# Retention on split fp32r operands, keys first, with the first norm computed beside the modulation

## The chip, the cores and the metric

The kernel runs on one core of one Trainium2 chip. The metric is the device time of one execution in microseconds (us). A run gives several executions, and their median counts.

## The reference

A four-layer diffusion-style model over 512 image tokens and 256 context tokens with 1024 features, all in fp32. Each layer has an adaptive modulation (six vectors from a conditioning vector), an RMS norm, a mixer, a second RMS norm and a gated feed-forward part. The mixer of layer 0 is windowed attention, that of layer 1 is bidirectional retention, those of layers 2 and 3 are mixed. The change touches the retention and the first norm of the program. Cut to these:

```python
h_x = modulate(rms_norm(x, norm1_g[i]), mx[0], mx[1])      # x * rsqrt(mean(x*x) + eps) * g, then h * (1 + scale) + shift
# retention, per head (4 heads, 256 key features, 512 value features), T = 512 image + 256 context tokens
q, k = rope_2d(q), rope_2d(k) * 256 ** -0.5                # context keys are not rotated
scores = einsum('bnhd,bmhd->bhnm', q, k) * decay           # forward and backward decay, gamma_h ** |n - m|
o = einsum('bhnm,bmhe->bnhe', scores, v)                   # keys and values of the image and of the context
mu = mean(o, -1); var = mean(square(o - mu), -1)
y = (o - mu) * rsqrt(var + EPS) * gn_gain
out = (silu(g) * y) @ w_o
```

## The kernel before, in words

Activations lie with features on the 128 partitions and tokens along the free axis. Weights come in units of 128x1024 (512 KB): the queue of SyncE loads unit u into `WR[u % 2]`, ScalarE rounds it to fp32r into `WH[u % 2]` (`refill`, line 684), VectorE takes the rest into `WL[u % 2]` (`refill`, line 1031), and TensorE multiplies. A product of a split weight and a split activation takes three fp32r passes, WH x HH, WH x HL, WL x HH (`product`, line 313; two outputs at once in `product_pair`, line 331; with activations as the stationary side and value rows as the outcome in `product_rows`, line 344). `refill(u)` on ScalarE waits for the load and for product u - 2, so each unit is split while the one before it is multiplied. Every engine runs its instructions in the order in which its program was written, with semaphores between them; this order is written out by hand in one function per engine.

**Retention** (lines 487, 852, 1257, 1550 for TensorE, ScalarE, VectorE, GpSimd) takes 16 units per head: 2 for the queries (512 tokens), 2 for the keys (768 tokens), 2 gates, 4 for the values (6 tiles of 128 tokens, 8 k steps), 2 gates, 4 for the output product. Keys and queries are rotated on VectorE (`rope`, six operations). Scores and values are plain fp32 matmuls: 12 for the scores (line 513) and 24 for the values (line 521), which the trace shows as two records each. VectorE multiplies the scores by the decay (line 1312) as it takes them out of PSUM. After the values ScalarE copies four tiles `rO` out, TensorE averages them over the features with a matrix of 1/512 (line 527, 4 fp32 matmuls), VectorE subtracts the mean (line 1315), ScalarE squares, TensorE averages the four squares (line 532, 4 matmuls), with the third gate's product between the two averages. Then come the fourth gate's product, the reciprocal root with a Newton step (`rsqrt` line 700, `newton` line 1080), the product with the gate on GpSimd (line 1555), the scaling (1322) and the split into `rYH` (ScalarE, 891) and `rYL` (VectorE, 1326), and the output product (line 548), whose result VectorE adds to X (line 1333, event `r_out`). The next head's first product waits for `r_out` of the last unit.

**First norm and modulation** (end of each program function). The first 4 x 2 pieces of the modulation weights, 1 MB each, are loaded into two buffers, a piece of part nb waiting for the matmul of part nb - 1 that read its buffer. X (3 MB) is loaded behind the first two pieces. After the fourth part TensorE turns the row results into columns (`ada_turn`), ScalarE squares the eight tiles of X, TensorE sums them as they come (line 388, 8 x 128x768 in fp32), and `norm` (lines 716 and 1086) follows: reciprocal root, Newton step, eight tiles scaled on VectorE (1108, 1111), modulated on ScalarE (725, 728, 732) and split on VectorE (1095, 1098). The first product pair takes the tiles as they come. In all later norms GpSimd sums the squares (line 1528) and TensorE takes two matmuls (line 382).

Of the kernel before, what the change touches and what calls it, by code (L numbers as in the profile page):

```python
# [6 lines left out]
ALU = mybir.AluOpType  # L7
ACT = mybir.ActivationFunctionType
F32 = mybir.dt.float32
# [5 lines left out]
P = 128  # L15
# [19 lines left out]
NB = 5 * P + 1  # L35

# [51 lines left out]
class Memory:  # L88
# [49 lines left out]
    def first_ada(self):  # L138
        t = self.tile
        self.AR0 = [t(f"AR0{i}", [P, 4, 512]) for i in range(2)]  # L140
        self.EV0 = t("EV0", [P, 512])
# [40 lines left out]
    def retention(self):  # L182
        t = self.tile
        self.rQ = t("rQ", [P, 2, S])
        self.rK = t("rK", [P, 2, T])
        self.rV = t("rV", [P, 6, 512])
        self.rG = t("rG", [P, 4, S])
        self.rO = t("rO", [P, 4, S])
        self.rAT = t("rAT", [P, 6, S])
        self.rYH = t("rYH", [P, 4, S], F32R)  # L190
        self.rYL = t("rYL", [P, 4, S], F32R)
# [6 lines left out]
        self.rDS = self.rO[:].rearrange("p a b -> p (a b)")[:, 0:NU]  # L198
        self.rTMP = self.rAT[:].rearrange("p a b -> p (a b)")[:, 0:NU]
# [46 lines left out]

HEADS = 6 * 16
# [62 lines left out]
def tensor_program(PE, M, on, FIRST):  # L310
    PS, HH, HL, WH, WL = M.PS, M.HH, M.HL, M.WH, M.WL

    def product(u, dst, src, nk, segs, after=None, ready=None, between=None):
# [5 lines left out]
        for k in range(nk):  # L319
            if between and k == 3:  # L320
                between()
# [22 lines left out]
    def product_rows(u, nk, k0, width, tiles, dst, first, last, ready=None, paired=False):  # L344

        PE.wait_ge(*on("w_lo", u))
        for at in range(nk * len(tiles)):
# [3 lines left out]
            for i, (h, w) in enumerate(((HH, WH), (HH, WL), (HL, WH))):  # L351
                mm = PE.matmul(dst(m), h[:, k0 + k, m * P:(m + 1) * P], w[u % 2][:, k * width:(k + 1) * width],  # L352
                               start=(first and k == 0 and i == 0 and not (paired and m % 2)),
                               stop=(last and k == nk - 1 and i == 2 and not (paired and m % 2 == 0)))
        mm.then_inc(*on.up("product", u))

    def ada_sum(l, nb, buf, before):
        for half in range(2):
            PE.wait_ge(*on(f"ada_load{half}", (l, nb)))
# [17 lines left out]
    def mean_square(tag, segs, summed):  # L377
        if summed:
            for i, t in enumerate((M.WK[2], M.WK[1])):
                PE.wait_ge(*(on("squared", (tag, KT - 1)) if i else on("square_summed", (tag, KT - 2))))  # L380
                for a, b, _ in segs:
                    mm = PE.matmul(PS[2][:, a:b], M.ONE[:, :], t[:, a:b], start=(i == 0), stop=(i == 1))
            mm.then_inc(*on.up("mean_square", tag))
            return
        for k in range(KT):
            PE.wait_ge(*on("squared", (tag, k)))
            for a, b, _ in segs:
                mm = PE.matmul(PS[2][:, a:b], M.ONE[:, :], M.WK[k % 2][:, a:b], start=(k == 0), stop=(k == KT - 1))
            if k < KT - 1:
                mm.then_inc(*on.up("square_taken", (tag, k)))  # L390
        mm.then_inc(*on.up("mean_square", tag))
# [95 lines left out]
    def retention():  # L487
        vb = [bank(PS, m) for m in range(6)]
        for h in range(4):
            u = FIRST["ret"] + 16 * h  # L490
            after = ("r_out", (h - 1, 3)) if h else None
            if h == 0:
                product_pair(u, PS, IMG, ("h_lo", "1a"))
            else:
                product(u, PS[0], (HH, HL), KT, IMG, after)
                product(u + 1, PS[1], (HH, HL), KT, IMG)
            product(u + 2, PS[2], (HH, HL), KT, ALL)
            product(u + 3, PS[3], (HH, HL), KT, ALL)
            for e in range(2):
                product(u + 4 + e, PS[e][:, 512:1024], (HH, HL), KT, IMG)  # L500
            PE.wait_ge(*on("r_rope", (h, 1)))
            PE.wait_ge(*on("r_gate", (h, 1)))
            for n in range(4):
                product_rows(u + 6 + n, 2, 2 * n, 512, range(6), lambda m: vb[m], n == 0, n == 3)
            for m in range(6):
                d = PS[(3, 0)[(m % 4) // 2]][:, 512 * (m % 2):512 * (m % 2) + 512]
                if m > 3:
                    PE.wait_ge(*on("r_decayed", (h, m - 4)))
# [1330 lines left out]
```

## Time and profile before

| | |
|---|---|
| median of 3 executions | 3689.19 us (3688.10 to 3695.85) |
| the profiled execution, its time | 3685.29 us |
| its span in the trace | 3684.0 us |
| granted TensorE clock, mean | 0.963 |
| TensorE matmuls busy | 3449.4 us (94%) |
| VectorE, ScalarE, GpSimd busy | 1743.7, 1214.7, 255.6 us |
| DMA | 334.24 MB, mean 91 GB/s |

The span runs from the first to the last instruction of the profiled execution; 1.3 us lie around it. A share of busy time is an average over all stages. The chain that ended last names, at each moment, the instruction on which everything behind it waited. Matmul records overlap: a pass that takes a new place every 0.2275 us has a record of 0.39 us, so stretches of the chain tell what a pass costs and the mean of a record does not.

### The profile page before, as it was taken

The page shows a single profiled execution, that of the slowest core. Times are in us where ns is not written, and L with a number is a line of the kernel's source. Part 1 is how long each engine was busy: PE and PEld are TensorE (multiplying, and loading weights), DVE is VectorE, ACT ScalarE, POOL GpSimd, SP SyncE. Part 2 cuts the span into 40 slices and gives each one's busy share as a digit, 9 for nine tenths or more (in the row PEclk, how much of TensorE's full clock was granted, in tenths as well). Part 3 has the DMA queues.
Part 4 walks back from the last instruction along what each step waited for, and adds up shares of the span by engine and source line. Part 5 has one row for each costly group of instructions (what it writes and reads, how often), then busy time and mean ns, then how long its engine had stood idle before and what let it go on. Part 6 is the DMA issues. An engine that isn't in the chain of part 4 may idle for free.

```text
span 3684.0 us, 42824 instructions
## 1 busy us (share of the span) xinstructions
PE 3449.4 (94%) x17952; PEld 2782.0 (76%) x17952; DVE 1743.7 (47%) x2627; ACT 1214.7 (33%) x1696; POOL 255.6 (7%) x337
## 2 busy tenths in 40 slices
PE   6979989999989999998999999889999989979998
PEld 3767778888865756656888786578888878568886
DVE  3567454333343333426757425546535433644343
ACT  4357442112232221224222424442212233543232
POOL 0101100000100000001001100010000010010001
PEclk7989999999999999999999998899999999889999
DMA  5400033323221211113544210023323322012222
GB/s 204 182 26 2 30 115 126 120 92 126 82 69 35 94 48 58 65 41 139 192 149 173 98 58 29 12 87 127 133 84 126 105 86 81 12 46 97 97 97 86
DMA packets 87776, 334.24 MB, mean 91 GB/s; under 512 B 11168, under 2 KB 14240, under 8 KB 83744
## 3 DMA queue, kind: packets, MB, share of 16 engines
q1 hardware_dynamic: 66416, 252.85, 19.3%
q0 software_dynamic: 21168, 78.65, 6.4%
q8 instruction: 142, 2.33, 0.2%
q14 instruction: 50, 0.41, 0.0%
HBM read 329.37 MB, written 2.10 MB: 90 GB/s over the span
## 4 chain that ended last, share of the span: by engine, by line
PE 89%; DVE 4%; ACT 4%; issue 1%; DMA 1%; SPq 0%; POOL 0%; DVEq 0%; ACTq 0%
PE PS L326 65%; PE PS L352 6%; PE PS L548 3%; PE PS L521 2%; PE PS L339 2%; PE PS L620 1%; PE PS L470 1%; PE PS L513 1%; PE PS L483 1%; PE PS L645 1%; PE PS L459 1%; PE PS L591 1%; DMA AR<-in_ada 1%; PE PS L632 1%; DVE dP L1450 1%
## 5 line engine op out<-in xcount | busy, mean ns | idle before, releaser
L692 ACT ACTIVATE WH<-WR 128x1024 fp32r<-128x1024 f32 (+1 forms) x376 | 419.0, 1115 | 1686.8 <-PE PS L326 1448.1
L326 PE MATMUL PS<-HH,WH 128*128 128x512 f32 (+1 forms) x3120 | 944.5, 358 | 29.7 <-DVE HL L1427 11.0
L326 PE MATMUL PS<-HL,WH 128*128 128x512 f32 (+1 forms) x3120 | 936.9, 355 | 0.0
L326 PE MATMUL PS<-HH,WL 128*128 128x512 f32 (+1 forms) x3120 | 936.6, 355 | 0.0
L1037 DVE TENSOR_TENSOR WL<-WR,WH 128x1024 fp32r<-128x1024 f32 (+1 forms) x376 | 486.0, 1293 | 928.6 <-ACT WH L692 928.2
L326 PEld LDWEIGHTS PS<-HH,WH 128*128 128x128 f32 x3120 | 514.6, 189 | 122.4 <-issue 16.6
L326 PEld LDWEIGHTS PS<-HL,WH 128*128 128x128 f32 x3120 | 514.4, 189 | 88.0 <-issue 2.2
L326 PEld LDWEIGHTS PS<-HH,WL 128*128 128x128 f32 x3120 | 513.9, 189 | 86.6
L326 PE MATMUL PS<-DH,WL 128*128 128x512 f32 (+1 forms) x1056 | 318.7, 356 | 0.0
L326 PE MATMUL PS<-DL,WH 128*128 128x512 f32 (+1 forms) x1056 | 318.7, 356 | 0.0
L326 PE MATMUL PS<-DH,WH 128*128 128x512 f32 (+1 forms) x1056 | 318.6, 356 | 0.0
L1163 DVE SCALAR_TENSOR_TENSOR X<-PS,MOD,X 128x512 f32<-128x512 f32 x96 | 60.6, 659 | 368.0 <-PE PS L326 368.0
L326 PEld LDWEIGHTS PS<-DL,WH 128*128 128x128 f32 x1056 | 174.2, 188 | 30.0
L326 PEld LDWEIGHTS PS<-DH,WL 128*128 128x128 f32 x1056 | 174.2, 188 | 30.0
L326 PEld LDWEIGHTS PS<-DH,WH 128*128 128x128 f32 x1056 | 174.1, 188 | 30.0
L1068 DVE SCALAR_TENSOR_TENSOR PS<-AT,CB 128x1024 f32<-128x1024 f32 x144 | 176.5, 1226 | 0.0
L352 PE MATMUL PS<-WH,HH 128*128 128x256 f32 (+1 forms) x416 | 142.2, 342 | 27.5 <-DVE HL L1095 15.8
L1536 POOL DMA_DIRECT2D AT<-in_adat x144 | 76.0, 528 | 1149.5 <-DVE AT L1068 574.7
L352 PE MATMUL PS<-WL,HH 128*128 128x256 f32 (+1 forms) x416 | 141.0, 339 | 0.0
L352 PE MATMUL PS<-WH,HL 128*128 128x256 f32 (+1 forms) x416 | 141.0, 339 | 0.0
L1528 POOL TENSOR_TENSOR WK<-WK,WK 128x768 f32<-128x768 f32 (+1 forms) x56 | 116.9, 2087 | 329.3 <-ACT WK L708 328.8
L767 ACT ACTIVATE DH<-WK 128x768 fp32r<-128x768 f32 (+1 forms) x88 | 65.1, 739 | 185.4 <-DVE WK L1154 185.4
(258 smaller groups left out, 3707.1 us busy)
## 6 DMA issues: line engine op xcount, KB each, us to landing
WR<-in_win SPq DMA_DIRECT2D x176, 512.0 KB, 3.5
AT<-in_adat POOLq DMA_DIRECT2D x144, 512.0 KB, 3.8
WR<-in_wdn SPq DMA_DIRECT2D x64, 704.0 KB, 4.0
WR<-in_wret SPq DMA_DIRECT2D x64, 512.0 KB, 3.6
WR<-in_zin SPq DMA_DIRECT2D x36, 512.0 KB, 3.5
AR<-in_ada SPq DMA_DIRECT2D x8, 1024.0 KB, 4.9
aV<-in_ada SPq DMA_DIRECT2D x8, 1024.0 KB, 4.9
aAR<-in_ada SPq DMA_DIRECT2D x8, 1024.0 KB, 6.5
```

Of the source, the lines that this page charges most:

```text
L326: mm = PE.matmul(dst[:, a:b], w[u % 2][:, k * P:(k + 1) * P], h[:, k, a:b], start=(k == 0 and i == 0), stop=(k == nk - 1 and i == 2))
L339: mm = PE.matmul(dst[v][:, a:b], w[(u + v) % 2][:, k * P:(k + 1) * P], h[:, k, a:b], start=(k == 0 and i == 0), stop=(k == KT - 1 and i == 2))
L352: mm = PE.matmul(dst(m), h[:, k0 + k, m * P:(m + 1) * P], w[u % 2][:, k * width:(k + 1) * width], start=(first and k == 0 and i == 0 and n ...
L521: mm = PE.matmul(d, M.rV[:, m, e * P:(e + 1) * P], M.rAT[:, m, :], start=(m == 0), stop=(m == 5))
L548: mm = PE.matmul(PS[half][:, 512 * v:512 * v + 512], wt[half][:, col:col + P], y[:, k, :], start=(k == 0 and i == 0), stop=(k == 3 and i = ...
L692: AC.activation(M.WH[u % 2][:, 0:n], M.WR[u % 2][:, 0:n], COPY).then_inc(*on.up("w_hi", u))
L767: AC.activation(M.DH[:, j, 0:n], HF[:, 0:n], COPY).then_inc(*on.up("d_hi", (l, jj)))
L1037: VE.tensor_tensor(M.WL[u % 2][:, 0:n], M.WR[u % 2][:, 0:n], M.WH[u % 2][:, 0:n].bitcast(F32), ALU.subtract).then_inc(*on.up("w_lo", u))
L1068: i = VE.scalar_tensor_tensor((PS[3], M.AT[v % 3])[j][:, :], M.AT[v % 3][:, :], 1.0, M.CB[:, j, :], ALU.mult, ALU.mult, accum_out=MOD[:, l ...
L1163: i = VE.scalar_tensor_tensor(X[:, m, a:b], PS[m % 2 if m else 2][:, a:b], MOD[:, l, 40 + m, j:j + 1], X[:, m, a:b], ALU.mult, ALU.add)
L1528: PO.tensor_tensor(WK[2][:, 0:n], WK[2][:, 0:n], WK[k % 2][:, 0:n], ALU.add).then_inc(*on.up("square_summed", (tag, k)))
L1536: PO.dma_start(M.AT[v % 3][:, :], dram["adat"][l - 1, v]).then_inc(*on.up(f"mod_load{v % 3}", (l, v), 16))
```

## The change

What it does, in the order of the work:

- **Keys first.** The units of a head start with the keys, into `PS[2]` and `PS[3]`, then the queries into banks 0 and 2, then two gates into banks 1 and 3. The first product of heads 1 to 3 waits for `r_gated` of the head before instead of `r_out`; the queries' products wait for `r_out`. In head 0 the pair that runs beside the norm is the keys' (768 tokens).
- **Three passes.** Rotated queries and keys, decayed scores and values are split into fp32r high and low parts, and scores and values are computed in 36 and 72 fp32r passes. The high parts are made on ScalarE, the low parts on VectorE.
- **Values centred at eviction.** ScalarE copies each value tile out with its row sum (`accum_out`), VectorE divides the sum by -512, ScalarE writes the centred high part, VectorE the low part. With centred values the outcome has mean zero over the features, so the average of line 527 and the subtraction of line 1315 are gone.
- **Order.** The third gate's product (u + 10) stands between scores and values; the fourth's (u + 11) follows the values, with the one variance matmul after its k = 4. ScalarE squares the four tiles straight from PSUM, VectorE adds them up; VectorE, not GpSimd, multiplies by the gate, from PSUM. The first output unit takes k in the outer place.
- **First norm.** Four modulation buffers in place of two (a load of part nb waits for part nb - 2). ScalarE squares X as soon as it is there, between the copies of the modulation parts; GpSimd sums the squares; TensorE takes the mean after the third part, before the fourth. VectorE scales five tiles before it finishes the modulation.

The core of the diff; lines taken away, which stand in the kernel above, are mostly left out, and so are the new buffers:

```diff
+RV_BANKS = (4, 5, 6, 7, 0, 2)
+RS_BANKS = (1, 3, 4, 5, 6, 7)
...
     def retention():
         for h in range(4):
+            out = lambda n: ("r_out", (h - 1, n)) if h else None
             if h == 0:
+                product_pair(u, PS[2:4], ALL, ("h_lo", "1a"))
             else:
+                PE.wait_ge(*on("r_gated", (h - 1, 3)))
+                product(u, PS[2], (HH, HL), KT, ALL)
+                product(u + 1, PS[3], (HH, HL), KT, ALL)
+            product(u + 2, bank(PS, 0), (HH, HL), KT, IMG, out(2))
+            product(u + 3, bank(PS, 2), (HH, HL), KT, IMG, out(3))
+            product(u + 4, bank(PS, 1), (HH, HL), KT, IMG)
+            product(u + 5, bank(PS, 3), (HH, HL), KT, IMG)
+            PE.wait_ge(*on("rK_lo", (h, 1)))
+            PE.wait_ge(*on("r_rope", (h, 0)))
             for n in range(4):
+                product_rows(u + 6 + n, 2, 2 * n, 512, range(6), lambda m: bank(PS, RV_BANKS[m]), n == 0, n == 3,
+                             event=(lambda m: ("v_rows", (h, m))) if n == 3 else None)
+            PE.wait_ge(*on("rQ_lo", (h, 1)))
             for m in range(6):
+                if m < 2:
+                    PE.wait_ge(*on("r_gate", (h, m)))
+                else:
+                    PE.wait_ge(*on("rV_raw", (h, m - 2)))
+                d = bank(PS, RS_BANKS[m])
                 for a in range(2):
+                    for i, (k, q) in enumerate(((M.rKH, M.rQH), (M.rKH, M.rQL), (M.rKL, M.rQH))):
+                        mm = PE.matmul(d, k[:, a, m * P:(m + 1) * P], q[:, a, :], start=(a == 0 and i == 0), stop=(a == 1 and i == 2))
                 mm.then_inc(*on.up("r_scores", (h, m)))
+            product(u + 10, bank(PS, 0), (HH, HL), KT, IMG, ("rV_raw", (h, 4)))
             for e in range(4):
+                d = bank(PS, RS_BANKS[e])
                 for m in range(6):
+                    if e == 0:
+                        PE.wait_ge(*on("rV_lo", (h, m)))
+                        PE.wait_ge(*on("rA_lo", (h, m)))
+                    for i, (v, a) in enumerate(((M.rVH, M.rAH), (M.rVL, M.rAH), (M.rVH, M.rAL))):
+                        mm = PE.matmul(d, v[:, m, e * P:(e + 1) * P], a[:, m, :], start=(m == 0 and i == 0), stop=(m == 5 and i == 2))
                 mm.then_inc(*on.up("r_values", (h, e)))
+            def variance():
+                if h == 0:
+                    PE.wait_ge(*on("step", "rON"))
+                PE.wait_ge(*on("r_square_sum", h))
+                PE.matmul(bank(PS, 6), M.rON[:, :], M.rSQ[:, 0, :], start=True, stop=True).then_inc(*on.up("r_var", h))
+
+            product(u + 11, bank(PS, 2), (HH, HL), KT, IMG, ("rV_raw", (h, 5)), None, variance, 5)
...
+                half, w = n % 2, u + 12 + n
+                PE.wait_ge(*on("w_lo", w))
+                PE.wait_ge(*(on("r_out", (h, n - 2)) if n > 1 else on("r_gate", (h, 2 + n))))
+                if n < 2:
+                    PE.wait_ge(*on("r_gated", (h, n)))
+                for at in range(8):
+                    v, k = (at % 2, at // 2) if n == 0 else (at // 4, at % 4)
+                    if n == 0 and v == 0:
+                        PE.wait_ge(*on("y_lo", (h, k)))
...
 def scalar_program(AC, M, on, FIRST, UNITS):
...
+            def high(what, a, dst):
+                AC.wait_ge(*on("r_half", (h, what, a)))
+                AC.activation(dst[:, a, 0:S], M.rST[a][:, :], COPY).then_inc(*on.up("r_hi", (h, what, a)))
+
+            refill(u + 2)
+            refill(u + 3)
             for a in range(2):
+                AC.activation(M.rKH[:, a, S:T], PS[2 + a][:, S:T], COPY).then_inc(*on.up("rK_ctx", (h, a)))
+            for a in range(2):
+                high(1, a, M.rKH)
+            refill(u + 4)
+            refill(u + 5)
+            for a in range(2):
+                high(0, a, M.rQH)
...
+            refill(u + 8)
...
+            refill(u + 9)
+            refill(u + 10)
+
+            def v_high(m):
+                AC.wait_ge(*on("rV_mean", (h, m)))
+                AC.activation(M.rVH[:, m, :], M.rVT[m % 2][:, :], IDENT, bias=M.rVM[:, m:m + 1]).then_inc(*on.up("rV_hi", (h, m)))
+
+            for m in range(6):
+                AC.wait_ge(*(on("v_rows", (h, m)) if m < 5 else on("product", u + 9)))
+                if m > 1:
+                    AC.wait_ge(*on("rV_lo", (h, m - 2)))
+                AC.activation(M.rVT[m % 2][:, :], bank(PS, RV_BANKS[m]), COPY,
+                              accum_out=M.rVM[:, m:m + 1]).then_inc(*on.up("rV_raw", (h, m)))
+                v_high(m)
+            refill(u + 11)
+            for m in range(6):
+                AC.wait_ge(*on("r_decayed", (h, m)))
+                AC.activation(M.rAH[:, m, :], M.rST[m % 2][:, :], COPY).then_inc(*on.up("rA_hi", (h, m)))
             refill(u + 12)
+            AC.activation(M.rG[:, 2, :], bank(PS, 0), ACT.Silu).then_inc(*on.up("r_gate", (h, 2)))
+            for e in range(4):
+                AC.wait_ge(*on("r_values", (h, e)))
+                AC.activation(M.rSQ[:, e, :], bank(PS, RS_BANKS[e]), SQUARE).then_inc(*on.up("r_squared", (h, e)))
+            rsqrt(("r", h), M.rVT[0][:, :], bank(PS, 6), M.rVT[1][:, :], ("r_var", h))
             refill(u + 13)
...
+    ada_copy(0, 0, M.EV0[:, :])
+    AC.wait_ge(*on("x_load", 0))
+    squares("0a", T, range(4))
+    ada_copy(0, 1, M.EV0[:, :])
+    squares("0a", T, range(4, KT))
+    ada_copy(0, 2, M.EV0[:, :])
+    root("0a", T)
+    ada_copy(0, 3, M.EV0[:, :])
     refill(0)
     refill(1)
...
 def vector_program(VE, M, on, FIRST, UNITS):
...
+            VE.wait_ge(*on("product", u + 1))
+            rope(h, 1, PS[2][:, 0:S], PS[3][:, 0:S], M.rKH, M.rKL)
+            for a in range(2):
+                VE.wait_ge(*on("rK_ctx", (h, a)))
+                VE.tensor_tensor(M.rKL[:, a, S:T], PS[2 + a][:, S:T], M.rKH[:, a, S:T].bitcast(F32),
+                                 ALU.subtract).then_inc(*on.up("rK_lo", (h, a)))
             refill(u + 4)
...
+            refill(u + 9)
+            refill(u + 10)
             for m in range(6):
+                VE.wait_ge(*on("rV_raw", (h, m)))
+                mean = M.rVM[:, m:m + 1]
+                VE.tensor_scalar(mean, mean, -1.0 / 512, None, ALU.mult).then_inc(*on.up("rV_mean", (h, m)))
+                VE.wait_ge(*on("rV_hi", (h, m)))
+                VE.scalar_tensor_tensor(M.rVL[:, m, :], M.rVT[m % 2][:, :], mean, M.rVH[:, m, :].bitcast(F32), ALU.add,
+                                        ALU.subtract).then_inc(*on.up("rV_lo", (h, m)))
+            refill(u + 11)
+            def low(m):
+                VE.wait_ge(*on("rA_hi", (h, m)))
+                VE.tensor_tensor(M.rAL[:, m, :], M.rST[m % 2][:, :], M.rAH[:, m, :].bitcast(F32),
+                                 ALU.subtract).then_inc(*on.up("rA_lo", (h, m)))
+
+            for m in range(6):
...
+                if m > 1:
+                    low(m - 2)
+                    VE.wait_ge(*on("rA_lo", (h, m - 2)))
                 VE.wait_ge(*on("r_scores", (h, m)))
+                VE.scalar_tensor_tensor(M.rST[m % 2][:, :], bank(PS, RS_BANKS[m]), 256 ** -0.5, mt, ALU.mult,
+                                        ALU.mult).then_inc(*on.up("r_decayed", (h, m)))
+            low(4)
+            low(5)
+            refill(u + 12)
+            def gated(e):
+                VE.wait_ge(*on("r_gate", (h, e)))
+                VE.tensor_tensor(M.rO[:, e, :], bank(PS, RS_BANKS[e]), M.rG[:, e, :], ALU.mult).then_inc(*on.up("r_gated", (h, e)))
+
+            SQ = M.rSQ
             for e in range(4):
+                VE.wait_ge(*on("r_squared", (h, e)))
+                if e:
+                    i = VE.tensor_tensor(SQ[:, 0, :], SQ[:, 0, :], SQ[:, e, :], ALU.add)
+                    i.then_inc(*(on.up("r_square_sum", h) if e == 3 else on.up("step", ("r_sum", h, e))))
+                    if e < 3:
+                        VE.wait_ge(*on("step", ("r_sum", h, e)))
+                if e < 3:
+                    gated(e)
+            newton(("r", h), M.rVT[0][:, :], bank(PS, 6), M.rVT[1][:, :])
             refill(u + 13)
             for e in range(5):
                 if e < 4:
+                    if e == 3:
+                        gated(3)
...
+        if modulation is not None:
+            first = 5
+            for k in range(first):
+                scaled(k)
+            modulation()
         for k in range(KT + 2):
+            if first <= k < KT:
+                scaled(k)
             if k > 1:
                 low(k - 2)
...
+    def first_modulation():
+        ada_finish(0, 1, 0, 4 * A0)
+        refill(0)
+        refill(1)
+
+    norm("0a", 0, 0, ALL, first_modulation)
...
 def tensor_program(PE, M, on, FIRST):
...
     for nb in range(A0):
+        ada_sum(0, nb, M.AR0[2 * (nb % 2):2 * (nb % 2) + 2], before_part(0, nb))
         ada_turn(0, nb, M.EV0)
+        if nb == A0 - 2:
+            mean_square("0a", ALL)
```

## Rows read from the trace of the kernel before

**Rows 1.** The page, part 4: shares of the span on the chain that ended last.
```profile
PE 89%; DVE 4%; ACT 4%; issue 1%; DMA 1%; SPq 0%; POOL 0%; DVEq 0%; ACTq 0%
```

**Rows 2.** Chain that ended last, head 1 of the retention: start us, us, what.
```profile
1216.78 39.00 PE PS L326 x192
1255.78 1.74 issue
1257.52 32.90 PE PS L352 x144
1290.42 10.32 PE PS L513 x24
...
1301.57 20.88 PE PS L521 x48
...
1323.13 3.70 PE PS L527 x8
...
1332.29 3.44 PE PS L532 x8
1335.72 5.46 PE PS L326 x24
...
1341.27 1.06 ACT WH L692
...
1342.42 1.23 DVE WL L1037
...
1345.01 1.65 DVE rYL L1326
...
1346.80 24.66 PE PS L548 x96
...
1371.48 1.42 DVE X L1333 x2
```

**Rows 3.** Timeline of GpSimd and of VectorE at the split of y, head 1.
```profile
1344.37 1.73 POOL L1555 TENSOR_TENSOR rO<-rO,rG 128x512 f32<-128x512 f32 x1 [7.59 <-ACT rG L888]
...
1347.23 0.68 DVE L1326 TENSOR_TENSOR rYL<-rO,rYH 128x512 fp32r<-128x512 f32 x1
```

**Rows 4.** Groups by line and shape, VectorE, GpSimd, ScalarE: busy us, mean ns.
```profile
L1312 DVE SCALAR_TENSOR_TENSOR rAT<-PS,rDC 128x512 f32<-128x512 f32 x16 | 10.3, 684 | 3.6 <-PE PS L513 3.6
L1111 DVE TENSOR_TENSOR TT<-X,RI 128x768 f32<-128x768 f32 x42 | 39.5, 952 | 0.0
L1528 POOL TENSOR_TENSOR WK<-WK,WK 128x768 f32<-128x768 f32 x35 | 79.7, 2278 | 247.2 <-ACT WK L708 247.2
L840 ACT ACTIVATION_READ_ACCUMULATOR aP<-aP,aNM 128x1 f32 x96 | 18.3, 190 | 0.0
```

**Rows 5.** Timeline of TensorE: the first pass of the layer-1 pair.
```profile
1054.46 0.77 PE L339 MATMUL PS<-HH,WH 128*128 128x512 f32 x1 [7.92 <-DVE HL L1095]
```

**Rows 6.** Chain that ended last, from the pair of layer 1 into the retention.
```profile
1068.24 0.97 PE PS L339 x3
...
1071.95 28.16 PE PS L326 x144
```

**Rows 7.** Chain that ended last, the first norm and its product pair.
```profile
40.12 1.88 PE PS L370 x8
...
42.92 12.78 PE PS L388 x32
...
59.52 1.15 DVE TT L1108 x2
...
63.61 19.09 PE PS L339 x96
```

**Rows 8.** Timeline of the DMA queue of SyncE: X is issued.
```profile
4.98 0.43 SPq L1617 DMA_DIRECT2D X<-in_xt  x1
```

**Rows 9.** DMA issues: engine, operation, count, KB each, median us to landing.
```profile
X<-in_xt SPq DMA_DIRECT2D x1, 3072.0 KB, 13.7
```

**Rows 10.** Timeline of TensorE: two fp32 matmuls after 3.75 us of idleness.
```profile
1688.61 3.28 PE L382 MATMUL PS<-WK,ONE 128*128 128x512 f32 x4 [3.75 <-POOL WK L1528]
```

More of the change, by code:

```diff
@@ L311, in tensor_program, with product @@
     PS, HH, HL, WH, WL = M.PS, M.HH, M.HL, M.WH, M.WL
-    def product(u, dst, src, nk, segs, after=None, ready=None, between=None):
+    def product(u, dst, src, nk, segs, after=None, ready=None, between=None, place=3):
         PE.wait_ge(*on("w_lo", u))
@@ L319, in product @@
         for k in range(nk):
-            if between and k == 3:
+            if between and k == place:
                 between()
@@ L524, in retention @@
-            if h == 0:
-                PE.wait_ge(*on("step", "rON"))
-            for e in range(4):
-                mm = PE.matmul(PS[0][:, 0:512], M.rON[:, :], M.rO[:, e, :], start=(e == 0), stop=(e == 3))
-            mm.then_inc(*on.up("r_mean", h))
-            product(u + 10, PS[3][:, 0:512], (HH, HL), KT, IMG)
-            for e in range(4):
-                PE.wait_ge(*on("r_squared", (h, e)))
-                mm = PE.matmul(PS[0][:, 512:1024], M.rON[:, :], M.rAT[:, e, :], start=(e == 0), stop=(e == 3))
@@ new lines, in retention @@
+            product(u + 11, bank(PS, 2), (HH, HL), KT, IMG, ("rV_raw", (h, 5)), None, variance, 5)
+            for n in range(4):
+                half, w = n % 2, u + 12 + n
[7 more added lines that the diff above has]
+                        PE.wait_ge(*on("y_lo", (h, k)))
+                    for i, (wt, y) in enumerate(((WH, M.rYH), (WH, M.rYL), (WL, M.rYH))):
+                        col = (v * 4 + k) * P
+                        mm = PE.matmul(PS[half][:, 512 * v:512 * v + 512], wt[w % 2][:, col:col + P], y[:, k, :],
+                                       start=(k == 0 and i == 0), stop=(k == 3 and i == 2))
+                mm.then_inc(*on.up("product", w))
@@ L1084, in newton, with norm @@
         VE.wait_ge(*on("rms", tag))
-    def norm(tag, l, which, segs):
+    def norm(tag, l, which, segs, modulation=None):
         n = segs[-1][1]
+        first = 0
         newton(tag, M.RI[:, 0:n], PS[2][:, 0:n], M.RS[:, 0:n])
@@ L1092, in low @@
             VE.wait_ge(*on("h_hi", (tag, k)))
-            if k == 0:
+            if k == 0 and modulation is None:
                 for a, b, j in segs:
@@ L1755, in layout @@
     for h in range(4):
+        parts.append(units(w[:, D + 256 * h + pair], KT))
         parts.append(units(w[:, 256 * h + pair], KT))
-        parts.append(units(w[:, D + 256 * h + pair], KT))
         parts.append(units(w[:, 4 * D + 512 * h:4 * D + 512 * h + 256], KT))
```

273 lines of the change are left out of this document (100 added, 173 removed).

## The prediction

> **What bounds the kernel now.** I read the chain that ended last first: TensorE carries 89% of the span [rows 1], so the change is worth what it takes off TensorE's queue and what it does to the waits in it. The same chain in order of time then gives one head of the retention as a list, 1216.78 to the next head's start [rows 2]: products (39.00), a pause (1.74), value rows (32.90), scores (10.32), values (20.88), two averages (3.70, 3.44), a stall before the output product, the output (24.66), and a wait for X. The reader is to see that each stretch begins where the one before it ends: nothing but TensorE's own work and these waits counts. Lastly the chain at the start [rows 7]: sums of squares (12.78), then some eight us until the pair starts at 63.61.
>
> **Unit prices.** A 512-column fp32r pass costs 5.46 / 24 = 0.2275 us, an fp32 matmul of that size 20.88 / 24 = 0.87 us [rows 2]. The keys' two products cost 39.00 - 96 x 0.2275 = 17.16, the queries' two 48 x 0.2275 = 10.92.
>
> **Per head, on TensorE's queue.**
> 1. Scores: 12 matmuls (10.32) become 36 passes (8.19). Gain 2.13, x4 = 8.5.
> 2. Values: 24 (20.88) become 72 passes (16.38). Gain 4.50, x4 = 18.0.
> 3. First average: 3.70 goes, and so does the wait for the copies ahead of it, 1323.13 - (1301.57 + 20.88) = 0.68. Gain 4.38, x4 = 17.5.
> 4. Variance: four matmuls (3.44) become one (0.87). Gain 2.57, x4 = 10.3.
> 5. Pause before the value rows, 1.74: they wait for the gate of bank 3 (PS[1] upper half) to be read. Now they go to banks whose readers, the key and query rotations, are covered by two gate products (10.9); the gates lie in banks 1 and 3, used by the scores. Gain 1.74, x4 = 7.0.
> 6. Wait of the values for the last decayed scores, 1301.57 - (1290.42 + 10.32) = 0.83: u + 10 (5.46) now stands between. Gain 0.83, x4 = 3.3, if the new splits are in time (below).
> 7. Turn of the head: 1.42 for X and a tenth for issue [rows 2]. Keys into PS[2] no longer wait for it; their units were split during the third output unit. Gain 1.5, three times = 4.5. The last turn leads into the norm and stays.
> 8. Stall before the output product: from the end of the fourth gate's product, 1335.72 + 5.46 = 1341.18, to 1346.80, 5.62 us. It is the split of u + 13 on ScalarE (1.06) and VectorE (1.23), which both queues have ahead of y, then y, its high and its low part. That order stays. But the low part took 1.65 against 0.68 for the next one, just while GpSimd multiplied its last gate [rows 2, 3]. The change takes that product from GpSimd; VectorE does it later, before y of tile 3. Gain 0.97, x4 = 3.9. The root chain has less cover: it was followed by a whole product and now by 3 of 8 k steps (2.05). Root, half and Newton I put at 2.8 together (four operations like that of line 1312, 0.684 [rows 4]), so 0.75 after the product's end; the split of u + 13 on VectorE begins 1.15 after it. Covered by 0.4.
>
> **Head 0.** The first pair takes the keys (768 tokens) while the norm delivers. The same shape took 19.09 at the first norm [rows 7], so from 1054.46 [rows 5] it ends at 1073.55; its first product half a step earlier, at 1072.5. The next product follows the first one's end by 1071.95 - (1068.24 + 0.97) = 2.74 [rows 6], so the queries start at 1075.2 and the gates at 1086.1, against 1071.95 + 17.16 = 1089.1. Gain 3.0.
>
> **What the splits add** beside TensorE: per head VectorE gets 18 tile operations for low parts and ScalarE about 22 activations. I followed both queues against TensorE's needs; a chained VectorE operation on a 512 tile counts 0.73 (0.684 [rows 4] and a hop, which I estimate at 0.04 from ScalarE's split ending at 1342.33 and VectorE's starting at 1342.42 [rows 2]).
> - Keys: a rotation is six operations behind the split of u + 3, so it ends 7 us after the keys' products, the low parts at 9; the weights of u + 4 are split at 10.1, needed at 10.9 (the queries' length). Slack 0.8. With the queries the slack is 1.2.
> - Values: per tile copy, accumulator read (0.19 [rows 4]), the small division, high part with a bias: 1.85 on ScalarE with the hops, against 1.37 in which TensorE delivers a tile (6 passes). Six tiles from 6.8 before the end of the value rows: the last high part comes 4.4 after it. The scores need only the first four evictions, u + 10 the fifth, at 8.2: hidden.
> - Decayed scores: VectorE starts them after the split of u + 11, at 6.8, and has 14 operations (6 decays, 6 low parts, 2 sums of decays), until 16.9. The values start at 8.19 + 5.46 = 13.65, and need the last tile after five of six, at 17.06. **Slack 0.15**, the tightest place. I cost it at nothing; if each operation took 0.1 more it would be 1.3 a head. Ends: 0 and 3 us a head.
> - Squares from PSUM and their sums end 1.4 after the values, the variance matmul comes 3.4 after: hidden. DVE's gate products (3 x 0.7) fit between tiles 4.1 apart.
> - DMA: same units, same order, and the wait of SyncE for `r_out` is unchanged, while u + 2 is wanted 6 us later than before.
>
> **First norm.** X lands at 5.0 + 13.7 = 18.7 [rows 8, 9], no longer of interest to the loads, which now run two parts ahead. GpSimd adds seven tiles at 2.28 [rows 4]: the sixth sum ends at 18.7 + 0.9 + 6 x 2.28 = 33.3, then the last square and the copy of part 2 behind it (1.5, an estimate: a scaling of such a tile took 0.95) and the turn (1.88 [rows 7]): 36.7. The mean is two matmuls of 768. After idleness 1024 columns took 3.28 [rows 10], so 1536 take 4.9: 41.6. From the mean's end to the first scaling it was 59.52 - (42.92 + 12.78) = 3.82: 45.4. Then five scalings of 0.95, which all stand ahead of the modulation: 50.2. Modulation (0.6), two weight splits (1.23 each) and the first low part (0.95): 54.0 for the start of the pair, against 63.61. The fourth part of the modulation is read and turned by 48, under the scalings. Gain 9.6. Bounds: 5, if the squares and copies hold each other up by one more part; 14, if GpSimd adds as fast as VectorE, or TensorE is at full clock. The Trainium skill (GPSIMD Engine Reference, section 3.1) gives about 2.6 cycles an element for such a sum, at 1.2 GHz an estimate of 1.66 us for 768; the seven sums would be 4.3 shorter, the total as much lower. The trace's 2.28 decides here.
>
> **Sum.** 8.5 + 18.0 + 17.5 + 10.3 + 7.0 + 3.3 + 4.5 + 3.9 = 73.0 for the heads, + 3.0 + 9.6 = 85.6. The profiled execution took 3685.3, with its span 1.3 less; 3599.7 for its like. The median of the runs lies 3.9 above it, which I leave in: **3603.6**.
>
> **Rivals.**
> - **The splits come late.** Place: decayed scores (slack 0.15) and the keys (0.8). If operations wait on each other's semaphores more than 0.04 us, TensorE stalls at the last tile of e = 0 and at u + 4, 3 us a head, +12: 3616. For: 14 chained operations. Against: their spacing in the rotation before was about 0.73, which is what I used. It cannot grow far: the chain is 10 us long, 30% is 3 us.
> - **The clock stays up in the stall of 4.65.** After 5.62 the output's 96 passes took 24.66, not 21.8: 2.8 more than warm passes take, which I read as the lower of the clock's two levels. If the shorter gap avoids it, up to -11: 3592. Against: after 3.75 us two fp32 matmuls took 3.28 where four take 3.44 [rows 2, 10].
> - **The first norm gives little.** With GpSimd, ScalarE and TensorE each waiting for parts of the other, 5 rather than 9.6: 3608, inside the range.
> - **The change is slower.** Mechanism: scores and values in groups that wait for a split tile each; TensorE runs in short pieces and its clock falls to half from scores to the fourth gate. 36 + 24 + 72 + 24 = 156 passes at 0.2275 more, 35.5 a head, 142 in all: 3746. It decides from a lateness of about 1 us per tile in both chains, so that the sixth is 6 us late; a total lateness of 21 us a head alone would also eat the gain. Against: only e = 0 waits per tile, the other 54 passes have all operands.
> - **The passes don't cost what others cost**, say fp32r operands made on the fly run like the fp32 pair (0.87): 108 x 0.64 x 4 = +277. The output product works on just such operands (rYH, rYL) at about 0.23 when warm [rows 2]; I give it 1%.
>
> **How the numbers follow.** My forecast, all terms within their bounds (3596 to 3610): 0.72. Splits late (3610 to 3622): 0.16. Clock stays up or the norm gains more (3585 to 3596): 0.09. Slower or no better: 0.03, of which 0.02 beyond 0.2%. A measurement of this kernel can tell 0.2% (7 us) from no change. The range 3590 to 3618 leaves out under 2 in 10.
>
> **What would show it.** In the chain of the changed kernel a head should take 137 to 139 us instead of 156: scores 8.2, values 16.4 without a wait, a variance of 0.87, no record of line 527, no pause before the value rows, a stall of 4.6 to 4.8 before the output product followed by passes of 0.43, none at the turn. The low part before that stall should take 0.7. The first pair should start at 54, with five scalings right ahead of the modulation on VectorE. Wrong would be: waits of TensorE for `rAL` or for `WL` of u + 4, passes of the scores away from 0.2275, or a first pair later than 58.

## The result, and the profile after

The changed kernel takes **3596.3 us** (median of 4, 3594.3 to 3596.8) against 3689.3 (4, 3688.1 to 3695.9): the ratio is 0.974, 95% interval 0.973 to 0.976. Forecast were 3603.6 and a range of 3590 to 3618. The profiled executions took 3596.15 with a span of 3594.8, and 3685.29 with 3684.0: 89.2 us, where the steps summed to 85.6.

The page after, part 4, the shares on the chain that ended last, as [rows 1]:

```profile
PE 90%; DVE 4%; ACT 4%; issue 1%; DMA 0%; POOL 0%; SPq 0%; DVEq 0%; ACTq 0%; POOLq 0%
```

The bound is what it was. The chain in order of time shows where the time went. Head 1 of the retention, as [rows 2] (start us, us, what):

```profile
1183.31 38.75 PE PS L344 x192
1222.05 32.65 PE PS L370 x144
1254.70 8.19 PE PS L526 x36
1262.89 5.47 PE PS L344 x24
1268.37 16.35 PE PS L536 x72
1284.72 3.43 PE PS L344 x15
1288.15 0.86 PE PS L543 x2
1289.01 2.07 PE PS L344 x9
...
1291.17 1.06 ACT WH L703
...
1292.33 1.23 DVE WL L1075
1293.55 0.68 DVE rO L1408
...
1294.25 0.64 ACT rYH L926
...
1294.91 0.70 DVE rYL L1412
...
1295.75 24.58 PE PS L558 x96
1320.33 1.74 PE PS L344 x10
```

From one head's start to the next it is now 1320.33 - 1183.31 = 137.02 us, where it was 1373.04 - 1216.78 = 156.26. Each stretch begins where its predecessor ends, from the keys (L344) over value rows (L370), scores (L526), a gate product, values (L536) to the variance (L543): the list has one gap left, the one before the output product, 4.67 us. No average of its own, no pause ahead of the value rows, no X at the turn.

The chain at the start, as [rows 7]:

```profile
4.97 14.06 DMA X<-in_xt
19.05 0.85 ACT WK L719
...
29.74 1.82 POOL WK L1617
...
32.34 0.59 ACT EV L709
...
32.97 1.87 PE PS L390 x8
34.84 5.34 PE PS L401 x8
...
44.06 4.43 DVE TT L1150 x5
...
48.98 2.36 DVE WL L1075 x2
51.34 0.88 DVE HL L1138
...
52.35 19.30 PE PS L357 x96
```

The first pair starts at 52.35, not 63.61. X, six of GpSimd's seven sums (29.74 is the start of the sixth), the turn of the modulation, the mean over 1536 columns (34.84) and five scalings follow each other as forecast. The seventh sum ends at 33.50, beside the copy and the turn.

### The profile page after: what moved, and what is told of

Read it like the earlier page. It is cut to its first block, busy times and chain, and to the rows that moved or that the text cites. A ratio compares the mean times of both kernels' runs of the same rounds, so it can differ in the third digit from the quotient of the medians.

```text
span 3594.8 us, 43191 instructions
## 1 busy us (share of the span) xinstructions
PE 3384.1 (94%) x18016; PEld 2798.3 (78%) x18016; DVE 1790.4 (50%) x2721; ACT 1255.0 (35%) x1781; POOL 247.6 (7%) x329
## 4 chain that ended last, share of the span: by engine, by line
PE 90%; DVE 4%; ACT 4%; issue 1%; DMA 0%; POOL 0%; SPq 0%; DVEq 0%; ACTq 0%; POOLq 0%
PE PS L344 67%; PE PS L370 6%; PE PS L357 3%; PE PS L558 3%; PE PS L536 2%; PE PS L630 1%; PE PS L481 1%; PE PS L494 1%; PE PS L655 1%; PE PS L470 1%; PE PS L526 1%; PE PS L601 1%; PE PS L642 1%; DVE dP L1536 1%; ACT aPT L850 1%
## 5 line engine op out<-in xcount | busy, mean ns | idle before, releaser
L344 PE MATMUL PS<-HH,WH 128*128 128x512 f32 (+1 forms) x3104 | 940.5, 357 | 24.6 <-DVE HL L1513 11.0
L344 PE MATMUL PS<-HL,WH 128*128 128x512 f32 (+1 forms) x3104 | 936.2, 356 | 0.0
L344 PE MATMUL PS<-HH,WL 128*128 128x512 f32 (+1 forms) x3104 | 934.7, 355 | 0.0
L344 PEld LDWEIGHTS PS<-HH,WH 128*128 128x128 f32 x3104 | 513.8, 189 | 114.5 <-DVE HL L1513 12.7
L344 PEld LDWEIGHTS PS<-HH,WL 128*128 128x128 f32 x3104 | 513.7, 189 | 86.0
L344 PEld LDWEIGHTS PS<-HL,WH 128*128 128x128 f32 x3104 | 513.3, 189 | 85.7 <-issue 1.2
L344 PE MATMUL PS<-DH,WH 128*128 128x512 f32 (+1 forms) x1056 | 319.0, 356 | 0.0
L344 PE MATMUL PS<-DH,WL 128*128 128x512 f32 (+1 forms) x1056 | 318.6, 356 | 0.0
L344 PE MATMUL PS<-DL,WH 128*128 128x512 f32 (+1 forms) x1056 | 318.5, 356 | 0.0
L344 PEld LDWEIGHTS PS<-DH,WH 128*128 128x128 f32 x1056 | 174.2, 188 | 30.1
L344 PEld LDWEIGHTS PS<-DL,WH 128*128 128x128 f32 x1056 | 174.3, 188 | 29.9
L344 PEld LDWEIGHTS PS<-DH,WL 128*128 128x128 f32 x1056 | 174.0, 188 | 30.0
L370 PE MATMUL PS<-WH,HH 128*128 128x256 f32 (+1 forms) x416 | 141.6, 340 | 20.5 <-DVE HL L1135 15.8
L1617 POOL TENSOR_TENSOR WK<-WK,WK 128x768 f32<-128x768 f32 (+1 forms) x63 | 129.4, 2054 | 343.4 <-ACT WK L719 342.1
L370 PE MATMUL PS<-WL,HH 128*128 128x256 f32 (+1 forms) x416 | 140.7, 338 | 0.0
L370 PE MATMUL PS<-WH,HL 128*128 128x256 f32 (+1 forms) x416 | 140.6, 338 | 0.0
```

What stands on the lines that cost most here:

```text
L344: mm = PE.matmul(dst[:, a:b], w[u % 2][:, k * P:(k + 1) * P], h[:, k, a:b], start=(k == 0 and i == 0), stop=(k == nk - 1 and i == 2))
L1617: PO.tensor_tensor(WK[2][:, 0:n], WK[2][:, 0:n], WK[k % 2][:, 0:n], ALU.add).then_inc(*on.up("square_summed", (tag, k)))
```

## The experiments

All but two (the first norm alone and the gate on VectorE) are made from the changed kernel. **The profile's stages are compared, not only totals**: below it turns out that stages which no edit touches differ by 2 to 5 us, from program to program and some of them between two executions of one program. The three experiments with one execution each (the turn, the multiplication, the slack) are read in their stages alone.

**Retention alone.** The changed kernel with the first norm as before (squares on GpSimd behind the load, loads one part ahead):

```
-            PE.wait_ge(*on(f"ada_load{2 * (nb % 2) + half}", (l, nb)))
+            PE.wait_ge(*on(f"ada_load{half}", (l, nb)))
-    squares("0a", T)
     attention()
     PO.wait_ge(*on("o_lo", (5, 1)))
...
```

> The retention of the changed kernel, the first norm and modulation of the kernel before. Sum theory: the two parts add up, so this run lies 73.0 + 3.0 = 76 us under the kernel before (3613), and the first pair starts at 63.6 again. Rival (pace): the passes of unchanged stages took a per cent more or less from run to run (feed-forward of layer 0 took 535.97 us before and 532.79 after), so 3 to 7 of the 89 us of span are not the change's; then this run shows the same retention, 137.4 a head, but a total that differs from the sum of its stages by some us.

Measured: 3610.1 us (4 executions), ratio 0.978 (0.976 to 0.980); a head takes 1331.33 - 1194.81 = 136.52.

**First norm alone.** The kernel before with only the norm's part of the change, the counterpart:

> The kernel before with the first norm and modulation of the changed one. Sum theory: the first pair starts at 52.4 instead of 63.6, total 9 to 11 under the kernel before (3679). Rival: the start gained is lost again in the attention that follows (there 1.5 us were lost in the changed kernel, where the second product took 9.93 instead of 8.59), and at the end of the attention at most 9 are left; a second rival, that the start hides behind the loads of weights, gives under 3.

Measured: 3678.6 us (10 executions), ratio 0.997 (0.996 to 0.999). Its chain at the mean and at the pair:

```profile
34.63 4.13 PE PS L385 x8
...
50.94 18.50 PE PS L343 x96
```

The pair starts 1.4 us earlier than was expected from the changed kernel, mostly because the mean took 4.13 us here and 5.34 there; more on this below.

What follows: the medians of the two, 78.9 and 10.4 us below the kernel before, add to 89.4; the whole change has 89.2 between the profiled executions and 93.0 between the medians. The parts add up as far as this can tell: the interval of the norm alone reaches from 5 to 15 us.

**The turn.** The keys of the next head wait for X again:

```
-                PE.wait_ge(*on("r_gated", (h - 1, 3)))
+                PE.wait_ge(*on("r_out", (h - 1, 3)))
                 product(u, PS[2], (HH, HL), KT, ALL)
```

> The changed kernel with one wait put back: the keys of heads 1 to 3 wait for r_out of the head before. Sum theory: a pause of 1.5 us at each of three turns, +4.5 in the span (3599), all else alike. Rival: the queue has other slack and the pause is absorbed by the splits of the next units being ready anyway, under +1.

The chain, from the end of head 1's output product into the next head:

```profile
1295.30 24.88 PE PS L558 x96
...
1320.21 1.42 DVE X L1419 x2
...
1321.67 8.39 PE PS L344 x46
```

The pause is back, 1321.67 - (1295.30 + 24.88) = 1.49 with its issue time, and the head takes 1321.67 - 1182.59 = 139.08, 2.06 more. The products behind the pause take 39.01 instead of 38.75. The last 0.3 are in the output product, 24.88 instead of 24.58; the changed kernel's own heads have anything from 24.19 to 25.00 there, so they are not the pause's. The total of the one execution was 3603.6, where 3599 was expected.

**The multiplication alone.** Scores and values as single fp32 matmuls, everything else of the change kept:

```
-                    for i, (k, q) in enumerate(((M.rKH, M.rQH), (M.rKH, M.rQL), (M.rKL, M.rQH))):
-                        mm = PE.matmul(d, k[:, a, m * P:(m + 1) * P], q[:, a, :], ...)
+                    mm = PE.matmul(d, M.rKH[:, a, m * P:(m + 1) * P].bitcast(F32), M.rQH[:, a, :].bitcast(F32), ...)
```

and the same for the values. It leaves the low parts out of both products.

> The changed kernel with scores and values as one fp32 matmul of the high parts each instead of three fp32r passes (the low parts are still made but not used, so the output has only the precision of the high parts). Sum theory: scores 10.3 instead of 8.2, values 20.9 instead of 16.4, so +6.6 a head, +26.5 in the span (3621). Rival (a pass depends on where its operands come from): another number than 0.87 per matmul; and if the splits were what bounds, the longer scores would hide them and less than +6.6 would show.

```profile
1260.17 10.30 PE PS L525 x24
1270.47 5.46 PE PS L344 x24
1275.93 20.60 PE PS L534 x48
```

10.30 and 20.60 against 8.19 and 16.35: the head takes 1332.51 - 1188.78 = 143.73, 6.71 more. Of 19.24 us a head a third is the three passes; the rest is what was taken out between them. The total of the one execution was 3626.3, where 3621 was expected.

**How much slack the decayed scores have.** Each low part computed twice, six operations of 0.7 us more in VectorE's chain:

```
                 VE.wait_ge(*on("rA_hi", (h, m)))
+                step(VE.tensor_tensor(M.rAL[:, m, :], M.rST[m % 2][:, :], M.rAH[:, m, :].bitcast(F32), ALU.subtract), ("twice", h, m))
```

> The changed kernel with the low part of each decayed score tile written twice, six more chained VectorE operations of 0.73, 4.4 us a head. By the forecast's slack (0.15 us at the last tile) TensorE would stall 4.2 us a head at the values, +17 in the span. By the trace of the changed kernel the low part of the last tile is done at 1269.7 and needed at 1268.37 + 5 x 0.68 = 1271.8, a slack of 2.1: a stall of 2.3 a head, +9. Rival: the scheme isn't bounded there at all, +0.

```profile
1271.16 0.61 DVE rAL L1364
1271.80 0.70 DVE rAL L1365
1272.50 0.14 issue
1272.64 13.19 PE PS L536 x57
```

Now TensorE's first 15 passes for the values run ahead and the other 57 wait for the low part of the last tile. The head takes 139.75, 2.73 more; six operations are 4.35, so some 1.6 to 2 us were free. The total of the one execution, 3618.2, lies 22 us above the changed kernel, where 9 (2.3 a head) or 17 (4.2 a head) were expected. From head 0's value rows to the end of the retention it is 11.7; another 12.5 lie in stages which the edit does not touch (5.8 in the attention of layer 2, 3.3 in the feed-forward behind it, 3.4 in layer 3), and up to head 0's value rows this execution was 3.5 ahead. The changed kernel itself shows the same slack. VectorE's timeline:

```profile
1268.21 1.47 DVE L1364 TENSOR_TENSOR rAL<-rST,rAH 128x512 fp32r<-128x512 f32 x2
```

and TensorE's, the first pass of the last tile:

```profile
1271.63 0.39 PE L536 MATMUL PS<-rAH,rVH 128*128 128x512 f32 x1
```

The last low part is there at 1269.68 and wanted at 1271.63: 1.95 us, not 0.15.

**Why the low part of y took 1.65 us.** The kernel before, with only the fourth gate's product moved from GpSimd to VectorE:

```
-            for e in range(4):
+            for e in range(3):
                 PO.wait_ge(*on("r_squared", (h, e)))
...
+                if e == 3:
+                    VE.wait_ge(*on("r_gate", (h, 3)))
+                    VE.tensor_tensor(M.rO[:, 3, :], M.rO[:, 3, :], M.rG[:, 3, :], ALU.mult)...
```

> The kernel before with one edit: the last of the four gate products of a head on VectorE instead of GpSimd. Theory (two engines at SBUF together): the low part ahead of the output product takes 0.7 instead of 1.65 and the stall 4.7 instead of 5.6, -0.95 a head, -3.8 in all (3685.5). Rival: the 1.65 is the price of the first of a row of such operations, and stays with GpSimd idle: 0.

Measured: 3688.2 us (10 executions), ratio 0.999 (0.999 to 1.000), nothing, where 3.8 us were expected. But VectorE's timeline of head 1 has the low part at its own length:

```profile
1345.22 0.69 DVE L1329 TENSOR_TENSOR rYL<-rO,rYH 128x512 fp32r<-128x512 f32 x1
...
1347.09 0.69 DVE L1322 TENSOR_TENSOR rO<-rO,rG 128x512 f32<-128x512 f32 x1
```

and TensorE's shows the stall shorter and a new one behind it:

```profile
1346.06 0.47 PE L548 MATMUL PS<-rYH,WH 128*128 128x512 f32 x1 [4.68 <-DVE rYL L1329]
...
1349.22 0.79 PE L548 MATMUL PS<-rYH,WH 128*128 128x512 f32 x1 [0.34 <-DVE rYL L1329]
```

1.65 became 0.69 and 5.62 became 4.68: GpSimd's product was the cause, and not the place as first of a row of such operations. In the old order of the output unit the third tile of y is wanted at the seventh pass, and its low part now stood behind the gate product and the fourth tile: the head took 157.17 against 156.26. The change walks its first output unit tile by tile over both halves, so that tile is wanted six passes later, and the changed kernel has no wait there; that the move is worth its 0.95 only with this order is concluded from the two traces, as no run has the new order without the move.

**The stall that is left.** The first three tiles of y need neither the weight tile's split nor the last gate, which were ahead of them in the queues. Here y comes first, the last gate after its second tile, the weights after its third, and the variance after three k steps instead of five:

```
-            product(u + 11, bank(PS, 2), (HH, HL), KT, IMG, ("rV_raw", (h, 5)), None, variance, 5)
+            product(u + 11, bank(PS, 2), (HH, HL), KT, IMG, ("rV_raw", (h, 5)), None, variance, 3)
...
-            refill(u + 13)
             for e in range(5):
+                if e == 4:
+                    refill(u + 13)
```

and the same on ScalarE, with the split behind the third high part.

> The changed kernel with the stall before the output product attacked: the variance matmul after k = 2 instead of k = 4, and the split of u + 13 behind the first three tiles of y on both queues, the fourth gate between tiles 1 and 2. Theory: the stall is made by the queue order. From the end of the values: variance 2.05 to 2.9, root and Newton to 5.75, y, high and low of tile 0 to 7.8, against 6.3 for the end of the fourth gate's product; the stall falls from 4.7 to about 1.5, the clock stays up (2.8 us), but tile 3 comes late and costs about 1.5 to 3 within the first output unit. Net -3 to -5 a head, 3577 to 3584. Rival: the table loads on ScalarE move into the chain and TensorE waits as long in the middle as it did at the start, so that only the clock's part or nothing is gained: 3585 to 3597.

Measured: 3588.0 us (5 executions), ratio 0.972 (0.971 to 0.974); a head takes 1315.77 - 1182.19 = 133.58, 3.44 less. The head is inside what was expected (3 to 5), the total is not (3577 to 3584): it fell into the rival's range (3585 to 3597), though the heads gained. So it was run again:

**Three kernels side by side on one chip**: the changed kernel unaltered, the last one again, and the last one with two operations of VectorE exchanged (the third tile's low part ahead of the fourth tile's y, the weights' low half last).

> The changed kernel unaltered, for a same-chip comparison with the two that follow and to tell whose the two durations of the first feed-forward are. If they belong to the execution, this profile shows either 532.8 or 536.0 us with equal chance, and single times spread over some 10 us round 3596 as those of the kernel before do round 3690. If they belong to the program (its addresses), it shows 532.8 again. Heads 137.0 us, pair at 52.4 us, either way.

> The kernel of e7 again, beside the changed kernel on one chip. Theory (the pause before the output product is the chain mean square, square root, two Newton steps, normalized tile, its two halves; the weight tile and the last gate stood in that chain without need): 3.44 us a head as in e7's trace, so 13.8 us below the changed kernel's median. Rival (e7's lower total came from its chip, the heads only trade the pause for later waits): under 5 us.

> e7 with the low half of the third tile computed ahead of the fourth tile's normalization, and the next weight tile's low half behind the fourth tile's. By e7's trace the third tile's low half would be done at 1294.83 instead of 1295.52 and the fourth's at 1296.9 instead of 1297.3: the first unit of the output product ends some 0.4 us earlier, 1.5 us in all over four heads. If the weight tile's low half, now last, ends after the first unit does (about 1298.0 against 1298.3), the gain is nothing or a small loss.

Measured: 3596.5 (5 executions, 3591.3 to 3599.0), **3583.7** (4, 3578.7 to 3589.2) and 3587.9 (4, 3581.8 to 3592.7). The second kernel's TensorE timeline at the output product:

```profile
1290.18 0.47 PE L558 MATMUL PS<-rYH,WH 128*128 128x512 f32 x1 [1.75 <-DVE rYL L1415]
1290.49 0.40 PE L558 MATMUL PS<-rYL,WH 128*128 128x512 f32 x1
...
1294.05 0.50 PE L558 MATMUL PS<-rYH,WH 128*128 128x512 f32 x1 [0.84 <-DVE rYL L1415]
```

The stall is 1.75 instead of 4.68, the passes behind it start 0.23 apart, and 0.84 come back in the middle of the first unit, where the third tile waits for its low part. The third kernel's head is 1315.31 - 1182.20 = 133.11, 0.47 better than 133.58, as expected, while its total reads 4.2 above the second's, inside both spreads. That the reordered kernel is faster than the changed one is shown (side by side its slowest execution, 3589.2, is below the other's quickest, 3591.3); by how much is less sure, 12.8 us between the medians here and 8.3 between those of the earlier occasions; which of the two orders is better in total is not shown. The changed kernel showed its 532.8 us again, as it should if they belong to the program; if they belonged to the execution, it was one chance in two (last section).

## Why the prediction was right

**The heads.** By the list of head 1, per head:

1. Scores: forecast 2.13; 10.32 to 8.19, 2.13.
2. Values: 4.50; 20.88 to 16.35, 4.53.
3. First average with its wait: 4.38, gone whole.
4. Variance: 2.57; 3.44 to 0.86, 2.58.
5. Pause before the value rows: 1.74, gone. The keys' and queries' readers were covered.
6. Wait of the values: 0.83, gone.
7. Turn: 1.5 three times; 1373.04 - (1346.80 + 24.66) = 1.58, and a pause of 1.49 with 0.26 behind it when the wait was put back alone.
8. Stall before the output product: 0.97; 5.62 to 4.67, 0.95, by the mechanism named: in the kernel before, moving the product alone took the low part from 1.65 to 0.69. The root chain stayed covered.

These make 18.72 of 19.24. The rest is pace: value rows 0.25 and products 0.25 less for the same passes, the output 0.08. No step had priced that. From the product behind head 0's pair (the keys' at 1071.95 before, the queries' at 1062.57 now) to the end of the last output it was 612.9 us and is 531.0, 81.9 less; by the steps it would be 76 and the 3.2 that head 0's larger pair gives back, 79.2.

**Head 0.** Forecast was a loss of 3.24 up to the product behind the pair, for the pair is now the larger one. The pair started 12.92 earlier, that product 1071.95 - 1062.57 = 9.38 earlier: 3.54.

**First norm.** 9.6 forecast, 11.26 at the pair. The mis-sized term is GpSimd's sum: 2.28 us from a mean over the whole kernel, 1.82 here, where VectorE has nothing to do (it stands idle for 29.00 us up to 42.08). Only six of the seven sums are on the chain; from the first one's start to the sixth one's end it is 31.56 - 19.97 = 11.6 where 13.7 were forecast: 2.1 less and not six times 0.46, since 0.14 lie between one sum and the next. X came 0.3 later and the mean cost 5.34, not 4.9, which takes a part back; the five scalings gave 0.3. (The forecast's own terms add to 54.2 for the pair, not 54.0.) The same Trainium skill section that the prediction weighed (GPSIMD Engine Reference, 3.1) gave an estimate of 1.66; the case lies nearer to it than to the row I chose. Over the whole changed kernel the mean is still 2.20, by the groups of GpSimd (busy us, mean ns):

```profile
L1617 POOL TENSOR_TENSOR WK<-WK,WK 128x768 f32<-128x768 f32 x42 | 92.3, 2197 | 267.5 <-ACT WK L719 266.7
```

The trace of the changed kernel puts the difference down to VectorE: the sums with VectorE idle took 1.80 to 1.82, one that began in the last 0.27 us of a split of weights on VectorE took 1.98 (at 1020.65), one that began 0.85 us before the end of such a split 2.55 (at 1009.36).

Of the 11.26, 1.3 are lost again until the attention ends: 9.93. Alone on the kernel before, the norm showed 13.7 there (406.69 to 392.95). Most of the difference is the granted clock of TensorE. From 37 to 40 us it was 0.50 in the changed kernel and 0.93 in the norm alone, and the mean took 5.34 and 4.13. From 87 to 90 it was 0.50 and 1.00, and the attention's product of 48 passes took 9.93 (at 88.61) and 8.43 (at 85.89), against 8.59 in the kernel before. It is not tied to the rest of the program: the run with the turn's wait, which has the changed kernel's first norm, had 0.95 from 37 to 40, a mean of 4.10 and its pair at 50.88. Over the nine traces with the new norm it is worth 8.8 to 15.3 us at the attention's end. What decides which clock these products get was not tried.

**The slack of 0.15 was wrong, without harm.** I had the decays begin 6.8 us after the value rows with 14 operations up to 16.9. They began 1.6 earlier, since an eviction of values took 1.61 per tile and not 1.85, and the chain took 9.7 instead of 10.15. So the rival that the splits come late had less to stand on than its 0.16. The keys' slack was nearer: the weights were split at 1210.10 (VectorE, 1208.89 and 1.21) and wanted at 1211.2, 1.1 instead of 0.8.

**The clock rival fell.** After the stall of 4.68 us the first ten passes of the output start 0.43 apart. The windows of TensorE in the changed kernel (us, PE busy (matmuls), granted clock, DMA share, GB/s):

```profile
1296.00:1298.00 2.00, 2.00 (x5) 0.50 0.10 39
...
1304.00:1310.00 6.00, 6.00 (x27) 1.00 0.26 86
```

A granted clock of 0.50 is the lower level, 1.2 GHz. The prediction put all that the output takes above 96 x 0.2275 = 21.8 down to it, 2.8 us. It is less: the ten slow passes take 4.36 (1295.75 to 1300.11), where the first ten of the reordered kernel take 2.41 (1290.18 to 1292.59), and the other 86 take 20.22, 0.235 each, at a granted clock of 1.00. So the lower level costs 2.0 us a head, and the rest is the output passes' own pace; the rival's -11 could have been -8 at most. Only after the 1.75 of the reordered kernel did the clock stay at 1.00. Of the 3.44 us a head that the reorder gave, 2.93 are the shorter stall; the output itself (1290.18 to 1314.25) is only 0.5 shorter, because the 2.0 that the full clock gives meet some 1.4 of new waits.

**The sum.** 85.6 against 89.2 in the profiled executions:

- start of the queries' products: 9.4, where the norm and head 0 were forecast at 6.4
- retention from there: 81.9 against 79.2
- after the retention: a loss of 2.1 against 0

Of the 9.4, 3.2 come from a feed-forward that no edit touches (last section); norm and head 0 alone gave 6.2. The loss of 2.1 is of the same kind: it is made up of stages that differ as much between two executions of the changed kernel (from the end of layer 2's attention to its feed-forward 97.75 and 95.58, against 95.67 before; in layer 3 144.40 and 146.89, against 146.64). So the steps were right for the stages that they name, heads above all; that the sum came within 3.6 us is in part luck, as 3.2 us of gain and 2.1 of loss come from stages that it does not name.

The 3.9 that I added for the median above the profiled execution were an error of method: they hold for the kernel before, whose profiled execution was a quick one, and the changed kernel's was at its own median. Without them it would have been 3599.7, 3.4 above the result and not 7.3. Between medians the gain is 93.0, 7.4 more than the steps.

## What to carry to other kernels

Where the chain is one engine's queue, list it stage by stage and price each stage from its own neighbours: eight terms of one head came out within 0.1 us, and two thirds of the gain were waits and helpers, not the faster multiplication. Take the price of a shared engine from a stretch where its neighbour is as busy as it will be, not from the mean of the kernel. And a move that shortens a wait must be followed to the consumer behind it: the same GpSimd product moved in the old order was worth nothing, and with the tile order changed 0.95 a head.

## What was not expected of the hardware

**A stage that nobody touched has one of two lengths, and which one seems to belong to the program.** The first feed-forward, 3072 passes, on the chain before and after:

```profile
506.92 535.97 PE PS L326 x3072
```

```profile
497.17 532.79 PE PS L344 x3072
```

The changed kernel showed 532.79 both times, on different occasions, as did the kernels with fp32 matmuls and with doubled low parts; before, both halves of the change, the turn's wait, the gate on VectorE and the reordered kernels (one of them twice, on two chips) 535.97 to 535.99. The stage by windows, before and then after:

```profile
510.00:560.00 50.00, 50.00 (x285) 1.00 0.40 138
...
660.00:710.00 50.00, 50.00 (x289) 1.00 0.37 126
```

```profile
500.00:550.00 50.00, 50.00 (x291) 1.00 0.43 137
...
650.00:700.00 50.00, 50.00 (x290) 1.00 0.39 126
```

At a granted clock of 1.00 and the same traffic the slow form lacks 5 or 6 passes in 50 us for some 150 us, then catches the other's pace. Likewise the differential attention of layer 2, from the end of its 32 products of L601 to the next product:

```profile
2150.13 13.97 PE PS L601 x32
...
2285.34 62.74 PE PS L344 x342
```

121.2 us in the changed kernel, both times (121.5 before, 123.6 in the retention alone), and 126.5 in the reordered one, both times:

```profile
2136.41 13.97 PE PS L601 x32
...
2276.86 62.26 PE PS L344 x342
```

So the reorder's 13.8 us in the heads appeared as 7.3 between two profiled spans (3595.3 and 3588.0), and as 12.8 between medians. What in a program selects the length was not tried.

Not every stage holds to its program. The feed-forward of layer 2, 3072 passes too, took 535.42 and 537.46 in two executions of the changed kernel, 535.48 and 538.17 in two of the reordered one. On top of that, executions of one program spread by up to 16 us (2.5 among the first four of the changed kernel, 16.3 among the ten of the norm alone), so an effect under 0.2% can be read only in its stage.
